# A fourth buffer for split weight panels, and other addresses for four tiles of the mixers

## What is computed

```python
def _layer(x, p_i, li, w_in, ...):
    h = x @ w_in                              # a_*, b_*, c_* of the three branches
    ya = moba_attention(...) * silu(a_z)
    qh, kvh = cq @ w_uq, ckv @ w_ukv          # the second branch has latents
    yb = mla_attention(...) * silu(b_z)
    yc = diff_attention(...) * silu(c_z)
    ga, gb, gc = split(sigmoid(x @ w_m + b_m))
    merged = ga * (ya @ w_a) + gb * (yb @ w_b) + gc * (yc @ w_c)
    r = ALPHA * x + merged @ w_o
    r = r + sigmoid(r @ w_pg) * (p_i @ w_p)
    return layernorm(r)
```

```python
u = modulate(rmsnorm(h), mod[0], mod[1])
h = h + 0.5 * (1 + mod[2]) * swiglu(u, wg, wu, wd)     # first feed-forward
u = modulate(rmsnorm(h), mod[3], mod[4])
rq, rk, rv, rg, sq, sk, sv, mz, mxbc, mdt = split(u @ w_in)
mixed = concat(retention(...), stick_breaking(sq, sk, sv), mamba2(...)) @ w_out
h = h + (1 + mod[5]) * mixed
u = modulate(rmsnorm(h), mod[6], mod[7])
h = h + 0.5 * (1 + mod[8]) * swiglu(u, wg, wu, wd)     # second feed-forward
```

## Time and profile before

| | us |
|---|---|
| runs shown | 1904.29, 1908.76, 1908.38 |
| median | 1908.38 |
| the profiled execution | 1908.42 |
| its span | 1907.1 |
| PE busy | 1821.1 (95%) |
| DVE busy | 1326.4 (70%) |
| ACT busy | 956.8 (50%) |
| casts L937, 306 | 542.5 |
| subtractions L943, 306 | 656.4 |
| mean granted clock | 0.973 |

### The profile page before, as it was taken

One profiled execution on the slowest core, in us unless ns is written; L12 is line 12 of the kernel. 1 busy time (PEld: TensorE's weight loads), 2 busy tenths in 40 slices (PEclk: granted clock), 3 DMA queues, 4 the chain that ended last, 5 costly groups with the idle time before them and its releaser, 6 DMA issues.

```text
span 1907.1 us, 34145 instructions
## 1 busy us (share of the span) xinstructions
PE 1821.1 (95%) x15048; PEld 1767.5 (93%) x15048; DVE 1326.4 (70%) x1807; ACT 956.8 (50%) x1322; POOL 62.6 (3%) x76
## 2 busy tenths in 40 slices
PE   7999999899999997999999899999999999999998
PEld 7998889799889997999999799999999999899998
DVE  5767677767677677766776867667766776867664
ACT  5655555447546545444465345445543456345443
POOL 0000100000010001000000110001000000010000
PEclk9999999899999998999899999999999899999998
DMA  8455356375454654567455435665566456335662
GB/s 316 186 213 202 131 209 241 131 281 192 151 224 149 225 217 185 193 257 266 178 213 207 155 130 201 257 254 219 199 256 255 173 201 243 122 145 182 252 254 107
DMA packets 59284, 389.70 MB, mean 204 GB/s; under 512 B 6656, under 2 KB 9472, under 8 KB 15232
## 3 DMA queue, kind: packets, MB, share of 16 engines
q1 hardware_dynamic: 59136, 387.52, 53.7%
HBM read 386.45 MB, written 1.05 MB: 203 GB/s over the span
## 4 chain that ended last, share of the span: by engine, by line
PE 71%; DVE 17%; ACT 8%; DMA 2%; issue 1%; POOL 0%; SPq 0%; DVEq 0%; ACTq 0%
PE banks L790 18%; PE banks L791 17%; PE banks L792 17%; DVE weights_split L943 7%; PE bank L791 4%; PE bank L790 4%; PE bank L792 4%; ACT weights_split L937 4%; DMA weights<-in_weights 2%; DVE weights L923 1%; DVE xbc L2414 1%; PE bank L863 1%; PE bank L876 1%; PE banks L993 1%; PE bank L1185 1%
## 5 line engine op out<-in xcount | busy, mean ns | idle before, releaser
L943 DVE TENSOR_TENSOR weights_split<-weights,weights_split 128x2048 fp32r<-128x2048 f32 (+3 forms) x306 | 656.4, 2147 | 323.9 <-ACT weights_split L937 322.6
L937 ACT CAST weights_split<-weights 128x2048 fp32r<-128x2048 f32 (+3 forms) x306 | 542.5, 1776 | 95.1 <-PE bank L792 70.4
L790 PE MATMUL banks<-u,weights_split 128*128 128x256 f32 (+1 forms) x1648 | 463.0, 281 | 7.6 <-DVE weights_split L943 4.3
L791 PE MATMUL banks<-u,weights_split 128*128 128x256 f32 (+1 forms) x1648 | 458.8, 278 | 0.0
L792 PE MATMUL banks<-u,weights_split 128*128 128x256 f32 (+1 forms) x1648 | 458.8, 278 | 0.0
L790 PE MATMUL banks<-x,weights_split 128*128 128x256 f32 x1056 | 305.5, 289 | 26.7 <-DVE weights_split L943 20.4
L790 PEld LDWEIGHTS banks<-u,weights_split 128*128 128x128 f32 (+1 forms) x1648 | 310.6, 188 | 10.2 <-DVE weights_split L943 4.7
L791 PEld LDWEIGHTS banks<-u,weights_split 128*128 128x128 f32 (+1 forms) x1648 | 310.9, 189 | 0.4
L792 PEld LDWEIGHTS banks<-u,weights_split 128*128 128x128 f32 (+1 forms) x1648 | 310.8, 189 | 0.4
L791 PE MATMUL banks<-x,weights_split 128*128 128x256 f32 x1056 | 299.5, 284 | 0.0
L792 PE MATMUL banks<-x,weights_split 128*128 128x256 f32 x1056 | 299.3, 283 | 0.0
(11 more groups left out here) (340 smaller groups left out, 2984.2 us busy)
## 6 DMA issues: line engine op xcount, KB each, us to landing
weights<-in_weights SPq DMA_DIRECT2D x262, 1024.0 KB, 6.4
weights<-in_ada SPq DMA_DIRECT2D x80, 1024.0 KB, 4.8
weights<-in_weights SPq DMA_DIRECT2D x36, 512.0 KB, 5.3
weights<-in_weights SPq DMA_DIRECT2D x4, 576.0 KB, 5.5
constants_second<-in_constants_second SPq DMA_DIRECT2D x1, 1792.0 KB, 10.0
weights<-in_weights SPq DMA_DIRECT2D x2, 640.0 KB, 7.4
h<-in_x SPq DMA_DIRECT2D x2, 512.0 KB, 5.3
out<-xbc SPq DMA_DIRECT2D x4, 256.0 KB, 2.2
```

Source lines behind the costliest of these rows:

```text
L790: pe.matmul(out, left[0], right[0], start=start, stop=False, **more)
L791: pe.matmul(out, left[0], right[1], start=False, stop=False, **more)
L937: act.do.copy(split[:, 0, 0:n], raw[:, 0:n]).then_inc(*self.act_wrote.inc(("weights", key)))
L943: dve.do.tensor_tensor(split[:, 1, 0:n], raw[:, 0:n], split[:, 0, 0:n].bitcast(F32), ALU.subtract).then_inc(*self.dve_wrote.inc(("weights" ...
```

## The change

The split buffers become four and `AHEAD` three. `pair` gets an argument, and the first gate panel of each feed-forward passes 2, so that its `use` prepares nothing; the `use` of the second gate panel then prepares two panels. In SBUF the fourth split buffer takes 16 KB of a partition. `r_k`, `r_g`, `m_z` and `r_v`, which only the mixers use, lie where the feed-forwards' `raw` lies; a small tile `raw_end` fills up the rest of it. The pad behind the last split buffer is left out, so that the tiles behind the split buffers move by 16384 bytes exactly.

```diff
-SPLIT_SLOTS = 3
-AHEAD = 2
+SPLIT_SLOTS = 4
+AHEAD = 3
...
-    def pair(self, name, l, i):
-
-        self.use((name, l, i))
+    def pair(self, name, l, i, ahead=AHEAD):
+
+        self.use((name, l, i), ahead)
...
-        self.pair("wg" + n, l, 0)
+        self.pair("wg" + n, l, 0, 2)
...
-            self.tile(f"space{i}", [P, 32])
+            if i < SPLIT_SLOTS - 1:
+                self.tile(f"space{i}", [P, 32])
...
-        b["raw"] = sb("raw", [P, DC, 2, T + 2], F32R)
+        with ExitStack() as feed_forward:
+            b["raw"] = self.tile("raw", [P, DC, 2, T + 2], F32R, feed_forward)
+        for n in ("r_k", "r_g", "m_z"):
+            b[n] = sb(n, [P, 4, T])
+        b["r_v"] = sb("r_v", [P, TB, 512])
+        sb("raw_end", [P, DC * 4])
...
-        for n in ("r_q", "r_k", "r_g", "m_z"):
-            b[n] = sb(n, [P, 4, T])
+        b["r_q"], b["s_v"] = sb("r_q", [P, 4, T]), sb("s_v", [P, TB, 512])
         b["y_r"] = b["r_q"]
-        for n in ("r_v", "s_v"):
-            b[n] = sb(n, [P, TB, 512])
```

## The result

The changed kernel is slower: 1914.49 us (median of 6 runs, 1909.21 to 1918.63) against 1906.09 us before (6 runs, 1904.29 to 1908.76), a ratio of 1.0041 with a 95% interval of 1.0029 to 1.0053, or some 8 us. The forecast was 1901.4, with a range from 1886 to 1912.

The account below looks back on a forecast made before the run. TensorE's own work plus its waits were taken as the bound. Gains of 3.4 (first block, early), 6.3 (output projection), 0.0 (feed-forwards) and -2.7 (mixers) gave 7.0 us, so 1908.4 became 1901.4, range 1886 to 1912.

Parts of the forecast that it names:

- The eleven panel waits: TensorE's waits for low parts of weight panels outside the start: all go, 19.7 us, or 27.5 with slow matmuls.
- The step that failed: Panel loads: the emptying subtraction moves by the same place, so each load finds its raw buffer free; cost nothing.
- 1.0 to 1.1: First block, early: gain in us kept of each 1.74 us wait, at 163.72 and its like in layer 1.
- rival C: Panel data come too late for the fourth buffer, first-block waits stay, 8.3 us of gain lost: 1909.7 us; chance 0.05.
- Forecast for the first block: Gain in both layers: 3.4 us from the early part and 6.3 from the output projection.
- Slow matmuls behind new waits: TensorE at the lower clock after a new wait: 1.7 us charged at layer 0's stick-breaking scores, bounds 0 and 2.8.
- Output projection: End of first block: longer cast and subtraction cost 1.95 us per layer; 3.9 and 2.4 kept, together +6.3.
- Feed-forwards: Start of all four: a second subtraction lengthens the chain by 2.29 us, waits move to the fourth gate panel; together 0.0.
- rivals B: No change: each new wait at the feed-forwards' fourth gate panel starts a slow stretch, 6.8 against 7.0, 1908.2 us; chance 0.15.
- D: Slower: a second cast also joins each feed-forward's chain, 4.7 us each, 18.8 in all, 1920.2 us; chance 0.13.
- Mixers: Chain before the stick-breaking scores 2.7 us later, scores start 0.8 later: -2.5 in layer 0, -0.2 in layer 1.

Follow-up runs that it names:

- pause: The changed kernel, loading no modulation rows in layer 0 while branch a is merged and branch b's latent products run: 1913.38 us, ratio 1.0033.
- short sums: First block's modulation sums cut to 64 of 1024 columns, loads untouched: 1905.83 us (0.9993) on the changed kernel, 1902.37 (0.9972) with two panels ahead everywhere.
- the version with the pauses: Changed kernel, three panels ahead only in the first block, modulation loads there paused in both layers from branch a's merging through latents, made up later: 1898.43 us, 0.9961.

## Why the prediction was wrong, point by point

*The eleven panel waits go*: right. The line for L943 fell to 9.3 us, the 8.6 and 0.7 of the start.

*The step that failed* is the one that costs the loads: "so each load finds its buffer free where it did before; I cost this at nothing", and with it "1.0 to 1.1" kept at the latents and nothing lost at branch c. The subtraction of a weight panel moves by a place, but the sum that empties the buffer of the modulation's rows, L923, does not move, and SP's queue goes in order through both. So a cast one further ahead stands there while its load still waits for that sum. I had that late panel as the prediction's rival C, with a chance of 0.05, and priced it as TensorE's panel waits that stay. What came is worse: the cast that waits blocks ScalarE, and copies behind it that TensorE needs. The term put at nothing shows as ScalarE's waits for panels, 46.0 us instead of 21.1, and as TensorE's for `b_q`, 5.5 instead of none. Forecast for the first block +9.7 us; in the profile it is -3.7, by the ratios about -2 (-1.9 with the second block at three ahead, -2.9 with it at two). The new waits for `b_q` (5.5 us) and for `y` of the branches (5.5), and slow matmuls behind them, are most of the profile's difference. That the sums on VectorE are what makes the copies late is shown (pause, short sums); how much of that goes through the late buffer, and whether the panels' sizes alone would have cost something in that place, is open.

*Slow matmuls behind new waits*: mis-sized. I charged 1.7 us once, at the scores. The windows show 1.7 at 309.36, 1.7 at 654.07, 3.0 at 999.90 and 2.0 at 1579.20 (34 in 5.80), together 8.4 and without those behind `b_q`, as much as the 7.8 that the old waits had cost. The 1.7 at 654.07 is of this profile: its wait of 3.36 us is shorter in the others.

*Output projection*, 1.95 us in each layer: right in place and size (waits of 2.28 for `y`), but it was no loss of its own, since undoing it only moved the wait to `x`.

*Feed-forwards*: right. Four waits of about 1.0 us for `u` (1.3 forecast), at full clock, and with the panel waits that went a small gain, 1.3 us in the profile, where 0.0 was forecast; the earlier trace rows's slack of 0.95 was used up as written. The prediction's rivals B and D had put their price here and fall.

*Mixers*: the mechanism was right, the size not. The scores start 0.5 us later than before relative to the stage's start in layer 0 (5.5 at 999.90 against 5.0 at its beginning; 0.8 forecast), with a wait of 4.14 (4.6 forecast) and 3.0 lost behind it (1.7 forecast). In layer 1, where I had charged no slow matmuls, they start 1.6 us later (8.3 against 6.7), with a wait of 4.03 and 2.0 lost behind it. Forecast -2.7 for both, in the profile -3.2 and -4.4. The run with two ahead there gives 5.7 us back.

So of the 17 us between forecast and profile (7.0 less against 10.2 more), 13.4 are the first block's (9.7 + 3.7), 4.9 the mixers' (7.6 against 2.7), and the feed-forwards came out 1.3 better. By the ratios after is 7.8 us slower, some 15 off the forecast: 11.6 of it the first block's (9.7 + 1.9), 3.0 the mixers' (5.7 against 2.7).

## What to carry to other kernels

A deeper ring at one stage is worth only what the ring ahead of it can feed: look at who empties the buffers that the loads go into, in the order of the loading queue, before buying depth further on. A preparation that is put earlier in an in-order queue costs twice if it has to wait there, since it holds up everything behind it; look for copies behind it that the bounding engine needs. And a wait of the matmul engine that is removed here and put there mostly took its slow stretch along (behind six of seven long ones here), so count that with both. Read a stage's loss from more than one profile: here one had 3.7 us where seven together gave 2.3.

## What the runs showed that I had not expected

The spread of a kernel's runs differs with its order: after ran from 1909.21 to 1918.63, the version with the pauses from 1897.94 to 1898.87. Where the slow stretches fell differed between profiles, too; why one order is so steady was not looked into. And a load of 1 MB whose median from issue to landing is 6.6 us in after took 8 in the burst of four from 171.08.
